# Eleven feed-forward "down" projections as seven block products a pair

## The reference

```python
# first block
up = jax.nn.relu(jnp.einsum('bsd,df->bsf', hn, w_mlp_up[l]))      # 1024 -> 4096
h = h + jnp.einsum('bsf,fd->bsd', up * up, w_mlp_down[l])          # 4096 -> 1024
# second block, two layers, each with two of these around its mixers
x = x + 0.5 * swiglu(rms_norm_2(x, ffn1_norm[l]), ffn1_w_gate[l], ffn1_w_up[l], ffn1_w_down[l])
def swiglu(h, w_gate, w_up, w_down):                               # 1024 -> 2816 -> 1024
    return (jax.nn.silu(h @ w_gate) * (h @ w_up)) @ w_down
```

## Time and profile before

| | |
|---|---|
| median of three runs | 3373.37 us |
| span of the profiled execution | 3368.4 us |
| what lies around the span, by the median | 5.0 us |
| TensorE busy | 3331.5 us, 99% |
| VectorE busy | 1936.8 us, 58% |
| ScalarE busy | 1332.8 us, 40% |
| GpSimd busy | 253.0 us, 8% |

### The profile page before, as it was taken

How to read it: one execution, slowest core, us unless ns; L and a number is a source line. 1 busy time by engine, 2 the same in 40 slices (tenths; PEclk the granted TensorE clock), 3 DMA queues, 4 the chain that set the end, 5 groups by cost and what they waited for, 6 DMA issues and landing times.

```text
span 3368.4 us, 42673 instructions
## 1 busy us (share of the span) xinstructions
PE 3331.5 (99%) x15738; PEld 2743.1 (81%) x15738; DVE 1936.8 (58%) x2682; ACT 1332.8 (40%) x1907; POOL 253.0 (8%) x302
## 2 busy tenths in 40 slices
PE   8999999999999999999999999999999999999999
PEld 6878887888888888778888888888887788888887
DVE  5777876464446544578654444453436975454444
ACT  4455435332224242445744322342324575442223
POOL 1000000000000000038200000000000760000000
PEclk9999999999999999999999999999999999999999
DMA  4333332233323333322222333333332232223332
GB/s 145 95 86 95 97 108 82 97 107 100 100 89 99 92 95 100 91 88 82 82 88 63 100 99 90 90 109 93 95 97 87 84 100 78 73 76 99 100 98 78
DMA packets 424749, 313.76 MB, mean 93 GB/s; under 512 B 15432, under 2 KB 421376, under 8 KB 424592
## 3 DMA queue, kind: packets, MB, share of 16 engines
q1 hardware_dynamic: 421264, 301.77, 29.9%
q0 software_dynamic: 2896, 8.49, 0.8%
q10 hardware_dynamic: 432, 1.38, 0.1%
HBM read 309.46 MB, written 2.13 MB: 93 GB/s over the span
## 4 chain that ended last, share of the span: by engine, by line
PE 90%; POOL 3%; issue 3%; DVE 3%; ACT 1%; DMA 0%; SPq 0%; POOLq 0%; ACTq 0%; DVEq 0%
PE G L735 78%; POOL arena L2818 2%; PE G L914 2%; PE G L891 2%; PE B L724 1%; PE G L676 1%; PE B L655 1%; PE B L914 1%; PE B L627 1%; PE G L936 1%; PE G L954 1%; PE G L724 1%; PE B L587 0%; DVE w_lo L2075 0%; PE G L1096 0%
## 5 line engine op out<-in xcount | busy, mean ns | idle before, releaser
L735 PE MATMUL G<-y_hi,w_hi 128*128 128x512 f32 x2272 | 895.1, 394 | 0.3 <-DVE w_lo L2075 0.2
L735 PE MATMUL G<-y_hi,w_lo 128*128 128x512 f32 x2272 | 884.7, 389 | 0.0
L735 PE MATMUL G<-y_lo,w_hi 128*128 128x512 f32 x2272 | 884.3, 389 | 0.0
L735 PE MATMUL G<-xn_hi,w_hi 128*128 128x512 f32 x1760 | 690.9, 393 | 0.8 <-DVE w_lo L2075 0.8
L735 PE MATMUL G<-xn_hi,w_lo 128*128 128x512 f32 x1760 | 685.1, 389 | 0.0
L735 PE MATMUL G<-xn_lo,w_hi 128*128 128x512 f32 x1760 | 684.9, 389 | 0.0
L1331 ACT ACTIVATE w_hi<-raw 128x1024 fp32r<-128x1024 f32 x319 | 337.6, 1058 | 729.1 <-PE G L735 648.4
L2075 DVE TENSOR_TENSOR w_lo<-raw,w_hi 128x1024 fp32r<-128x1024 f32 x332 | 412.6, 1243 | 345.9 <-ACT w_hi L1331 329.3
L1333 ACT ACTIVATE w_hi<-raw 128x1024 fp32r<-128x1024 f32 x256 | 272.1, 1063 | 761.1 <-PE G L735 761.1
L735 PEld LDWEIGHTS G<-y_hi,w_hi 128*128 128x128 f32 x2272 | 426.5, 188 | 98.1 <-issue 9.0
L735 PEld LDWEIGHTS G<-y_lo,w_hi 128*128 128x128 f32 x2272 | 426.6, 188 | 91.7 <-issue 4.3
(11 more groups left out here) (484 smaller groups left out, 3414.6 us busy)
## 6 DMA issues: line engine op xcount, KB each, us to landing
raw<-in_w_in SPq DMA_DIRECT2D x128, 512.0 KB, 4.4
raw<-in_ffn_w_gate SPq DMA_DIRECT2D x88, 512.0 KB, 4.0
raw<-in_ffn_w_up SPq DMA_DIRECT2D x88, 512.0 KB, 5.2
raw<-in_ffn_w_down SPq DMA_DIRECT2D x64, 512.0 KB, 4.0
raw<-in_w_mlp_up SPq DMA_DIRECT2D x32, 512.0 KB, 4.6
raw<-in_w_mlp_down SPq DMA_DIRECT2D x32, 512.0 KB, 4.3
raw<-in_xa_wkv SPq DMA_DIRECT2D x32, 512.0 KB, 4.4
raw<-in_w_out SPq DMA_DIRECT2D x24, 512.0 KB, 3.9
```

The source lines that it names most:

```text
L735: m = pe.matmul(bank[:, 0:n], a[:, k, kt, :], b[:, kt * S:kt * S + n], start=(kt == tiles[0] and t == 0), stop=(kt == tiles[-1] and t == 2))
```

## The change

Eleven phases (`BLOCKED`: down0 to down2 and, in both layers and both feed-forward layers, the first two of the three "d" parts) compute each pair as block products. The weight of a pair is seen as a 2 x 2 matrix of blocks (even or odd tiles of input channels by the two panels of 128 output channels) and the activations as a 2 x 2 matrix (even or odd tiles by the two halves of 256 tokens). Four block sums of weights and four of activations ("mixes") replace the eighth product, by Winograd's form of Strassen's scheme.

- Each of the seven products is 4 tiles x 3 matmuls of 256 columns. Banks x, y, z and "extra" collect them; ScalarE copies x into y and z as a seed between products, and VectorE evacuates 256 columns at a time, six times a pair.
- Of the weight block sums S1 and S3 are made by GpSimd, S2 and S4 by VectorE. Each of the seven weight operands gets its high part from ScalarE and its low part from VectorE, 512 elements each, through four slots of `w_hi` and `w_lo`; the slot of a product is free when the product four before it is done. A pair's last operands are made while it is being multiplied.
- In the phase before, VectorE forms the four mixes of each two activation tiles (256 columns each), ScalarE their high part, VectorE their low part, into `m_hi` and `m_lo`. The last pair of that phase has a body of its own, which also makes the first operands. These phases and the blocked ones are unrolled on ScalarE and VectorE, the blocked ones on TensorE too.
- `angles` and `sines` move from `f1d01` to the swiglu phase `f1u02`; `memory` stays in `f1d00`.

In order: the new functions of TensorE, ScalarE and VectorE for a blocked phase, VectorE's body for the last pair of a swiglu phase, and GpSimd's sums. `first_operands` 0 to 3 are: low part A11 and sum S2; low part S1; low part S2; low part A12.

```diff
+            def blocks(name, after=None):
...
+                for i in range(4):
+                    n, every = P0[name] + i, range(nk // 2)
...
+                    x, y, z, extra = accumulators(name, i)
+                    pe.wait_ge(op_v.sem, op_v.at(name, i, A11))
+                    product(i, FIRST, x, every, True)
+                    pe.wait_ge(op_v.sem, op_v.at(name, i, S1))
+                    if i:
+                        pe.wait_ge(gone_v.sem, gone_v.at(name, i - 1, "q22"))
+                    product(i, MIX1, extra, every, True)
+                    pe.wait_ge(op_v.sem, op_v.at(name, i, S2))
+                    pe.wait_ge(seed_a.sem, seed_a.at(name, i, "y"))
+                    if i:
+                        product(i, MIX2, x, every, False)
+                        pe.wait_ge(op_v.sem, op_v.at(name, i, A12))
+                        product(i, SECOND, y, every, False)
+                    else:
+                        product(i, MIX2, x, every[:-1], False)
+                        pe.wait_ge(op_v.sem, op_v.at(name, i, A12))
+                        product(i, SECOND, y, every[:-2], False)
+                        product(i, MIX2, x, every[-1:], False)
+                        product(i, SECOND, y, every[-2:], False)
...
+                    pe.wait_ge(op_v.sem, op_v.at(name, i, S3))
+                    pe.wait_ge(seed_a.sem, seed_a.at(name, i, "z"))
+                    product(i, MIX3, z, every, False)
+                    pe.wait_ge(op_v.sem, op_v.at(name, i, S4))
+                    product(i, THIRD, x, every, False)
+                    pe.wait_ge(s_wlo, 2 * n + 2)
+                    pe.wait_ge(gone_v.sem, gone_v.at(name, i, "z"))
+                    product(i, MIX4, z, every, False)
...
+            def blocks(name, more=None):
+                for i in range(4):
+                    n = P0[name] + i
+                    if i:
+                        operand_hi(name, i, A12)
+                        seed(name, i, "y")
+                    operand_hi(name, i, S3)
+                    if i == 0:
+                        mix_hi(name, KTS[name] // 2 - 1, D14, last_mix(name))
+                    operand_hi(name, i, S4)
+                    seed(name, i, "z")
+                    operand_hi(name, i, A22)
+                    for x in range(3):
+                        if i < 3:
+                            operand_hi(name, i + 1, (A11, S1, S2)[x])
+                        else:
+                            next_half_hi(name, x)
...
+            def blocks(name, scale, more=None):
...
+                for i in range(4):
+                    x, y, z, extra = accumulators(name, i)
+                    if i:
+                        last_of(i - 1)
+                        operand_lo(name, i, A12)
+                        operand_sum(name, i, S4)
+                    operand_lo(name, i, S3)
+                    if i == 0:
+                        operand_sum(name, 0, S4)
+                        mix_value(name, KTS[name] // 2 - 1, D14, last_mix(name), *last_tiles(name))
+                    dve.wait_ge(block_p.sem, block_p.at(name, i, MIX1))
+                    evacuate(i, extra, 0, 1, 1.0, None).then_inc(gone_v.sem, gone_v.mark(name, i, "q12"))
+                    operand_lo(name, i, S4)
+                    evacuate(i, extra, 1, 1, -1.0, None).then_inc(gone_v.sem, gone_v.mark(name, i, "q22"))
+                    operand_lo(name, i, A22)
...
+                    dve.wait_ge(block_p.sem, block_p.at(name, i, SECOND))
+                    evacuate(i, y, 0, 0, 1.0, None).then_inc(gone_v.sem, gone_v.mark(name, i, "y"))
+                    if i < 3:
+                        operand_lo(name, i + 1, A11)
+                        operand_sum(name, i + 1, S2)
+                    else:
+                        next_half_lo(name, 0)
+                    dve.wait_ge(block_p.sem, block_p.at(name, i, MIX3))
+                    evacuate(i, z, 1, 1, -1.0, "q22").then_inc(gone_v.sem, gone_v.mark(name, i, "z"))
...
+                        operand_lo(name, i + 1, S1)
...
+                    dve.wait_ge(block_p.sem, block_p.at(name, i, THIRD))
+                    evacuate(i, x, 0, 1, 1.0, "q12").then_inc(gone_v.sem, gone_v.mark(name, i, "x"))
...
+                        operand_lo(name, i + 1, S2)
...
+                    if last:
+                        even, odd, values = tmp(3 - q), tmp(2 + q), ffn_mix(q)
+                        mix_value(down, i // 2, D12, values, even, odd)
+                        first_operands(down, 0) 
+                        mix_lo(down, i // 2, D12, values)
+                        first_operands(down, 1)
+                        dve.wait_ge(s_free, n)
+                        product(n, 0)
+                        dve.tensor_tensor(tmp(q), G[2 * q][:, :], rstd[:, :], ALU.mult).then_inc(s_ao, 1)
+                        product(n, 1)
+                        dve.tensor_tensor(tmp(4 + q), G[2 * q + 1][:, :], rstd[:, :], ALU.mult).then_inc(s_free, 1)
+                        first_operands(down, 2)
+                        dve.wait_ge(s_free, n + 1)
+                        dve.wait_ge(s_yh, 2 * i + (BASE[name][1] + 1))
+                        dve.tensor_tensor(odd, tmp(4 + q), tmp(q), ALU.mult).then_inc(s_ao, 1)
+                        dve.wait_ge(s_ao, 2 * i + (BASE[name][0] + 2))
+                        for kind_ in (D12O, D32):
+                            mix_value(down, i // 2, kind_, values, even, odd)
+                        first_operands(down, 3)
+                        mix_lo(down, i // 2, D12O, values)
+                        dve.wait_ge(s_yh, 2 * i + (BASE[name][1] + 2))
+                        lo_of(cut(inner_of(name)[1], i), odd, cut(inner_of(name)[0], i)).then_inc(s_yl, 1)
+                        mix_lo(down, i // 2, D32, values)
...
+            def block_sums(names_):
+                for name in names_:
+                    for i in range(4):
+                        n, nk = P0[name] + i, KTS[name]
+                        if (name, i) != (BLOCKED[0], 0):
+                            before = (name, i - 1) if i else (BLOCKED[BLOCKED.index(name) - 1], 3)
+                            pool.wait_ge(op_v.sem, op_v.at(*before, S1))
+                        pool.wait_ge(s_load[n % 2], LANDED[n])
+                        for m, a, b in ((S1, quarter(n, 0, 1, nk), quarter(n, 1, 1, nk)), (S3, quarter(n, 0, 1, nk), quarter(n, 0, 0, nk))):
+                            pool.tensor_tensor(operand(n, m, nk), a, b, ALU.add).then_inc(sum_p.sem, sum_p.mark(name, i, m))
```

More of the change, by code:

```diff
@@ L157, in at @@
         return Signal.marks.get((self.name, key), 1)
+HALF = S // 2
+BLOCKED = [f"down{_p}" for _p in range(3)] + [f"{_f}d{_l}{_i}" for _l in range(2) for _f in ("f1", "f2") for _i in range(2)]
+BEFORE_BLOCKED = {PHASES[_i][0]: PHASES[_i + 1][0] for _i in range(len(PHASES) - 1) if PHASES[_i + 1][0] in BLOCKED}
+A11, S1, S2, A12, S3, S4, A22 = range(7)
+FIRST, MIX1, MIX2, SECOND, MIX3, THIRD, MIX4 = range(7)
+D12, D12O, D32, D14 = range(4)
 def cut(t, i, n=S):
@@ L1361, in body @@
                     first = r is not None and isinstance(i, int) and i == 0
+                    down = BEFORE_BLOCKED.get(name)
+                    last = down and isinstance(i, int) and i == NPAIR[name] - 1
+                    if last:
+                        operand_hi(down, 0, A11)
+                        operand_hi(down, 0, S1)
+                        square(0)
+                        mix_hi(down, i, D12, mlp_mix(i))
+                        operand_hi(down, 0, S2)
+                        operand_hi(down, 0, A12)
+                        seed(down, 0, "y")
+                        square(1)
+                        mix_hi(down, i, D12O, mlp_mix(i))
+                        mix_hi(down, i, D32, mlp_mix(i))
+                        return
                     prep(n, q, landed, 0)
@@ L1369, in body, with swiglu @@
                     square(1)
-                loop_pairs(act, name, body, peel=0 if r is None else 2)
-            def swiglu(name, r=None):
-                def body(i, n, q, landed):
+                    if down:
+                        for kind_ in (D12, D12O, D32, D14):
+                            mix_hi(down, i, kind_, mlp_mix(i))
+                loop_pairs(act, name, body, peel=0 if r is None else 2, unroll=name in BEFORE_BLOCKED)
+            def swiglu(name, r=None, more=None):
+                def body(i, n, q, landed):
+                    down = BEFORE_BLOCKED.get(name)
+                    last = down and i == NPAIR[name] - 1
+                    if last:
+                        operand_hi(down, 0, A11)
+                        operand_hi(down, 0, S1)
+                        mix_hi(down, i // 2, D12, ffn_mix(q))
+                        act.wait_ge(s_ao, 2 * i + (BASE[name][0] + 1))
+                        act.activation(tmp(q), tmp(q), ACT.Silu).then_inc(s_yh, 1)
+                        operand_hi(down, 0, S2)
+                        operand_hi(down, 0, A12)
```

(20 more changed lines are left out.)

284 lines of the change are left out of this document (262 added, 22 removed).

## The result

The changed kernel takes 3381.03 us (median of 8 runs, 3375.55 to 3382.85) where the kernel before took 3373.02 on the same chips: ratio 1.0024, 95% interval 1.0014 to 1.0034. It is slower by 8 us. The prediction said slower by 17.6: the side is right, the size is more than double.

A forecast was written before the change was run, and what follows sets the result against it. TensorE, busy 99% of the span, was taken to set the time alone. Terms -36.4 + 20 + 21 + 8 + 5 = +17.6; 3368.4 + 17.6 + 5.0 = 3391.0 us, own range 3378 to 3408, 8 in 10: 3354 to 3427.

The forecast's parts named there:

- The step that failed is the steady pair's wait for bank z: Second and third pairs: GpSimd's sums hold VectorE, so TensorE waits 0.5 us each before the seventh product.
- The gain: Blocked pairs: 84 matmuls of 256 columns replace 48 of 512, sparing TensorE 0.83 us a pair, -36.4 us in all.
- The first pair's seam: First pair of a phase: TensorE waits 1.9 us for the seed of z before its fifth product, +21 us.
- its z wait: First pair of a phase: VectorE is late from the start, and TensorE waits 0.8 us for bank z.
- The MLP: Seams of the three MLP phases: tile 6 late by 2.3, with small waits 2.7 us a phase, +8 (0 to 12).
- The memory work: f1d0 part 0: 9.3 us of operations on a VectorE with almost no free time, half taken, +5 us (0 to 9).
- The unrolled loops, the angles, SP's queue and the convolution sums: Unrolled code, angles in f1u02, SP's loads, GpSimd's later sums: each taken as 0, the unrolled loops up to +3 us.
- The clock: Half-clock spells after TensorE's seam stalls: taken as 0; +9 us were one to follow every second stall.
- The no-change case: Seam as forecast, z wait a third, MLP and memory half: -1 us, 3372 us; chance 0.19.
- "Faster": VectorE keeps ahead, the order hides the seam to 1 us a phase, no z wait: -20, 3353 us; chance 0.18.

The follow-up runs named there:

- run 7: The changed kernel with GpSimd multiplying the weight blocks instead of adding them in its sums; ratio 1.0016 to the kernel before.
- Run 4: The changed kernel with each S1 sum made twice on GpSimd (S1 twice); ratio 1.0107 to the kernel before.
- run 1: The changed kernel with ScalarE's seed of bank z put before the high parts of D14 and S4 in each phase's first pair; ratio 0.9997 to the kernel before.
- runs 3: The changed kernel with ScalarE's seed of z earlier in first pairs and VectorE's evacuation of z earlier in every pair; 3359.1 us, ratio 0.9962.
- run 10: The changed kernel with seed and evacuation of z earlier, and in first pairs that evacuation also before A22, D14 and y; 3352.7 us, ratio 0.9946.
- 11: The kernel of run 10 with f1d0 part 0, the phase with the memory work, as before the change; 3347.9 us, ratio 0.9930.
- run 8: The changed kernel with down0 to down2 as before the change and the eight FFN phases blocked; ratio 1.0004 to the kernel before.
- z first: The changed kernel with VectorE's evacuation of bank z, in every pair, before low part A11 and sum S2; ratio 1.0002 to the kernel before.

## Why the prediction was right about the side and wrong about the size

**The step that failed is the steady pair's wait for bank z** (0.5 in the second and 0.5 in the third pair, 11 us of the 20; measured 1.5 in all, f1d00's among it). VectorE in the second pair of f2d01 in the changed kernel, and GpSimd beside it:

```profile
2094.29 1.29 DVE L2338 TENSOR_TENSOR w_lo<-raw,w_hi 128x512 fp32r<-128x512 f32 x1 [0.41 <-ACT w_hi L1571]
2095.50 0.41 DVE L2400 SCALAR_TENSOR_TENSOR h<-G,h 128x256 f32<-128x256 f32 x1
2095.83 1.45 DVE L2338 TENSOR_TENSOR w_lo<-raw,w_hi 128x512 fp32r<-128x512 f32 x1
...
2099.67 0.41 DVE L2400 SCALAR_TENSOR_TENSOR h<-G,h 128x256 f32<-128x256 f32 x1
```

```profile
2093.42 1.61 POOL L3260 TENSOR_TENSOR arena<-raw 128x512 f32<-128x512 f32 x1 [14.17 <-DMA raw<-in_ffn_w_down]
2094.99 1.74 POOL L3260 TENSOR_TENSOR raw<-raw 128x512 f32<-128x512 f32 x1
```

The mechanism is as forecast: S1 holds the low part S3, S3's sum holds the low part S4, the evacuation between goes on. But the holds are 0.60 and 0.76 (1.29 and 1.45 less 0.69), not 0.9 and 1.1. From the pair's first matmul at 2091.72, the low part S3 ends at 3.86 (forecast 3.95), the low part S4 at 5.56 (6.0), the evacuation of z at 8.36 (8.95), and TensorE wants the bank at 8.55 (8.62). A forecast wait of 0.5 became a margin, and the trace shows one of 0.19: z is out of its bank at 2100.08, and TensorE's seventh product starts at 2100.27. The largest part of the error is the price of a sum, taken from multiplications that had VectorE beside them: 1.48 for what takes 1.28 alone (run 7). The forecast let each sum wait for VectorE first and then take 1.48, and so had that wait in it twice, an estimated 0.4 of the 0.64 us by which the two holds were too long. At a threshold such an error does not scale the term, it removes it. Run 4 shows the other side of that threshold, 0.73 a pair for one sum more.

By the Trainium skill (SBUF — State Buffer, "Who interferes with whom") the loser of the port blocks for the whole instruction. The runs agree with the block: an addition more on GpSimd is a hold more on VectorE, and none on the evacuations between. What VectorE loses is nearly what is left of GpSimd's operation when its own one starts: 0.60 us of 0.74, and 0.76 of 0.90 (the rows above).

**Step by step.** The gain: 40.0 for 36.4, the pace 118.7 ns for 119.7. The first pair's seam: 2.07 for 1.9 (from the phase's first matmul at 2078.88 the seed is made at 7.66, forecast 7.65), and its z wait 0.68 for 0.8; the chain through VectorE and ScalarE was followed rightly, and run 1 shows that it is the chain and not its last link. The MLP: the tile's wait 1.66 to 1.87 and 0.3 of small ones for 2.7. The memory work: f1d00 waits 8.0 where 8.7 was the sum of its terms. In all the waits were to be 54 and were 39.9, 9.5 of the difference being the steady pairs and 3.4 the z wait of the first pair (0.68 in eight phases for 0.8 in eleven). The unrolled loops, the angles, SP's queue and the convolution sums cost nothing, as taken: the account leaves 0.4 us for them together.

**The clock** was taken at 0, with 9 as its bound, and it is a second miss, of the other sign. Three of eleven seam waits were followed by a spell of 3.4 us at half clock, 5 us; the other 6.8 stand in code that the change does not touch. That is why the profiled execution shows +12 where the waits (39.9) and the gain (40.0) alone cancel. Over all timed runs the clock is some 4 of the 8 us. So the prediction had the right side by luck: with its waits as they were and its clock at 0, it would have said no change.

**The rivals.** The no-change case came nearest with its terms, a third of the z wait (7 us; measured some 7) and MLP and memory at half, and gave 3372; the clock is the largest of what lies between it and 3381. "Faster" was right in what it needed, an order that hides the seam; the change did not have that order, and runs 3, 10 and 11 do: 3359, 3353 and 3348. Two engines' queues in one pair of every phase decide between +8 and -18 us (run 10).

## What to carry to other kernels

Where an added step makes an engine late by a queue of operations, follow the queue to its end before blaming the operation for which the bound engine is seen waiting: moving that one moves the wait. Put first what releases the bound engine and behind it what only the next stage needs, in both queues at once. And an operation given to GpSimd is not off VectorE's hands while VectorE's own operations have both inputs in SBUF: where VectorE is busy at that moment, price it as if VectorE did it (0.60 to 0.76 a sum here, for 0.61), where it is idle, as free. Take a forecast wait that is smaller than its own uncertainty as a case of its own, not as a term.

## What the hardware showed that was not expected

- GpSimd's addition and its multiplication of 128x512 both take 1.28 us alone, and 1.74 when they come upon a running VectorE operation: the lock delays both sides, GpSimd until VectorE's operation ends, VectorE until GpSimd's does. The operations seen going on beside GpSimd are those with an input in PSUM (0.41). Two inputs in SBUF is not the exact condition for being held: L1898 of the kernel before, one tensor and a column of scalars, took 1.52 us beside GpSimd, where the median of that line is 0.41.
- The clock after short waits: in the changed kernel and the twelve variants, 86 blocked phases have a longest TensorE wait of 2.06 us or more, and 31 of them have a spell of 3.4 us at half clock; the 51 phases whose longest wait is 1.89 or less have none. In 21 of the 31 TensorE had worked for 85 us or more without a pause over 1 us before the wait that the fall followed; in nine, MLP phases, another pause lay 3 to 5 us ahead of it, and in one 15. What decides in which of the 86 the clock falls is open (run 8 has 8 such phases and no fall in them, S1 twice 11 and 8 falls), and so is why the stages that are the same in all these kernels show from 0 (z first) to 17 us of it (changed).
- In the changed kernel a phase with such a spell shows no z wait behind the seam (2.07 alone in f1d01, where f2d01 has 2.07 and 0.68), and it takes 43.69 us for 42.81: 0.9 us more, where half of the spell is 1.7. The slower TensorE gives the late VectorE time to catch up.
